# Decoder-trunk step: last eight gelu chunks gated in PSUM and used first, x issued behind the silu, second norm's column sum ahead of three modulation rows

## The reference

```
mod = silu(c) @ w_mod + b_mod                       # six vectors of 1024 for each of 9 sequences
h   = RMSNorm(x) * (1 + scale1) + shift1
x   = x + gate1 * (mixer(h) @ w_out)                # short convolution and mLSTM heads
h   = RMSNorm(x) * (1 + scale2) + shift2
# PEER: 8 heads pick 16 of 128*128 single-neuron experts each, by product keys
a   = einsum(u_tab[picked], h)
y   = einsum(gelu(a) * gate, v_tab[picked])
out = RMSNorm(x + gate2 * y)
```

## Time and profile before

| what | value |
| --- | --- |
| median of 3 runs | 1741.51 us |
| profiled execution | 1741.11 us, span 1739.4 us |
| TensorE busy | 1680.4 us, 97% of the span |
| VectorE, GpSimd, ScalarE busy | 68%, 65%, 38% |
| mean granted TensorE clock | 0.985 |
| DMA | 467.58 MB, mean 269 GB/s |

### The profile page before, as it was taken

One profiled execution on the slowest core, in us unless ns is written; L12 is line 12 of the kernel. 1 busy time (PEld: TensorE's weight loads), 2 busy tenths in 40 slices (PEclk: granted clock), 3 DMA queues, 4 the chain that ended last, 5 costly groups with the idle time before them and its releaser, 6 DMA issues.

```text
span 1739.4 us, 27374 instructions
## 1 busy us (share of the span) xinstructions
PE 1680.4 (97%) x10559; PEld 1609.5 (93%) x10559; DVE 1180.1 (68%) x2322; ACT 667.0 (38%) x1063; POOL 1122.3 (65%) x676
## 2 busy tenths in 40 slices
PE   7999999798999999989999999999999999999996
PEld 3899888596999999989999999998999999999996
DVE  4340244635678789999887788445888888878855
ACT  2454213233334333333343334344444444444432
POOL 1767322121334888977666766776989799999962
PEclk9999999799999999999999999999999999999998
DMA  8645223123223899979999999998999999999951
GB/s 270 213 153 158 73 74 108 45 86 133 74 74 108 276 297 292 330 269 330 354 342 348 346 353 342 342 382 317 406 399 405 365 401 405 404 404 403 403 204 64
DMA packets 197314, 467.58 MB, mean 269 GB/s; under 512 B 21696, under 2 KB 103616, under 8 KB 197056
## 3 DMA queue, kind: packets, MB, share of 16 engines
q1 hardware_dynamic: 82176, 245.46, 40.3%
q0 software_dynamic: 46080, 167.79, 25.6%
q10 hardware_dynamic: 68928, 52.57, 9.1%
HBM read 410.78 MB, written 54.97 MB: 268 GB/s over the span
## 4 chain that ended last, share of the span: by engine, by line
PE 48%; DVE 4%; DMA 4%; POOL 1%; issue 1%; ACT 0%; SPq 0%; DVEq 0%; ACTq 0%
PE ps L896 43%; PE ps L907 5%; DMA tab<-in_tab 2%; DMA gate_scratch<-stage 1%; DVE ug L1522 1%; POOL tLo L640 1%; DMA gt<-gate_scratch 0%; DVE ps L1532 0%; DVE yo L1765 0%; POOL ug L650 0%; DMA gelu_scratch<-ga 0%; DVE eqb L1634 0%; DVE rs L1763 0%; DVE pick L1621 0%; ACT tHi L1142 0%
## 5 line engine op out<-in xcount | busy, mean ns | idle before, releaser
L640 POOL TENSOR_TENSOR tLo<-tab,tHi 128x1024 fp32r<-128x1024 f32 x256 | 621.5, 2428 | 172.0 <-ACT tHi L1142 169.2
L1142 ACT CAST tHi<-tab 128x1024 fp32r<-128x1024 f32 x256 | 268.1, 1047 | 287.1 <-PE ps L896 179.5
L896 PE MATMUL ps<-hHi,tLo 128*128 128x384 f32 x1024 | 351.6, 343 | 2.2 <-ACT ga L1197 1.5
L896 PE MATMUL ps<-actHi,tLo 128*128 128x384 f32 x1024 | 343.3, 335 | 5.5 <-issue 2.9
L896 PE MATMUL ps<-hHi,tHi 128*128 128x384 f32 x1024 | 345.1, 337 | 0.0
L896 PE MATMUL ps<-hLo,tHi 128*128 128x384 f32 x1024 | 344.1, 336 | 0.0
L896 PE MATMUL ps<-actLo,tHi 128*128 128x384 f32 x1024 | 342.7, 335 | 0.0
L896 PE MATMUL ps<-actHi,tHi 128*128 128x384 f32 x1024 | 342.7, 335 | 0.0
L628 POOL TENSOR_TENSOR wLo<-raw,wHi 128x1024 fp32r<-128x1024 f32 x53 | 127.8, 2411 | 309.5 <-ACT wHi L978 309.5
L1522 DVE SCALAR_TENSOR_TENSOR ug<-ug,ps 128x1024 f32<-128x1024 f32 x160 | 191.0, 1218 | 52.7 <-DMA ug<-in_urows,eidx 51.7
L1197 ACT ACTIVATE ga<-ps 128x384 f32<-128x384 f32 x128 | 62.8, 491 | 384.8 <-PE ps L896 374.2
(11 more groups left out here) (346 smaller groups left out, 2471.1 us busy)
## 6 DMA issues: line engine op xcount, KB each, us to landing
tab<-in_tab SPq DMA_DIRECT2D x256, 512.0 KB, 6.6
raw<-in_w SPq DMA_DIRECT2D x101, 512.0 KB, 3.8
gelu_scratch<-ga ACTq DMA_DIRECT2D x128, 192.0 KB, 5.8
gate_scratch<-stage ACTq DMA_DIRECT2D x48, 512.0 KB, 8.4
gt<-gate_scratch SPq DMA_DIRECT2D x32, 768.0 KB, 7.6
gin<-gelu_scratch SPq DMA_DIRECT2D x128, 192.0 KB, 10.2
ug<-in_urows,eidx POOLq DMA_INDIRECT x160, 6.7
ug<-in_vrows,eidx POOLq DMA_INDIRECT x160, 7.7
```

What stands on the lines that cost most here:

```text
L640: pool.tensor_tensor(tLo[:, n % SPL], tab[:, n % TABS], tHi[:, n % SPL].bitcast(F32), ALU.subtract).then_inc(s_tlo, 1)
L896: last = mm(ps[:, bank, 0:TD], w, x[:, k, 0:TD], start=first, stop=end)
L1142: nc.scalar.copy(tHi[:, n % SPL], tab[:, n % TABS]).then_inc(s_thi, 1)
```

## The change

Three places are edited.

1. At the start ScalarE first waits for the conditions c and applies the silu, and issues the four transfers of x behind it. TensorE's wait for the two constants moves from ahead of the first `mod_rows` to behind the second.
2. In the second norm `square_sum(1)` moves from behind `mod_columns(20)` to behind `mod_rows(20)`; on ScalarE `rms(1)` moves ahead of `mod_rows_out(21)`.
3. The last eight chunks (120 to 127) become the first group of the second half. Their gelu is written straight to PSUM bank 4 or 5, and `act_32` works on it there: for them no store, no load and no `gelu_copy`. The other 120 chunks follow in order. The host rolls the groups of `v_tab` by one, and the gate rows are read with an offset. Product 128 no longer waits for a whole group: its matmuls with k wait for `s_alo` 1 + k, and it waits for `s_gelu` NCH + 1 only. SyncE waits for the stores of 120 chunks instead of 128.

```diff
             pe.wait_ge(s_silu, 1)
             for m in range(NMA):
                 mod_rows(m)
+                if m == 1:
+                    pe.wait_ge(s_const, 2)
...
             mod_rows(NMS)
+            square_sum(1)
             mod_rows(NMS + 1)
             mod_columns(NMS)
-            square_sum(1)
...
-            def product(n, hi_in, lo_in, bank):
+            def product(n, hi_in, lo_in, bank, ready=None):
...
+                    if ready is not None:
+                        pe.wait_ge(s_alo, ready + k)
...
-            pe.wait_ge(s_gelu, NCH + 2)
+            pe.wait_ge(s_gelu, NCH + 1)
             for n in range(NCH, NT):
                 g = (n - NCH) // GRP
-                if n % GRP == 0:
+                if n % GRP == 0 and g:
                     pe.wait_ge(s_alo, GRP * (g + 1))
...
-                product(n, actHi[g % 2], actLo[g % 2], late_bank(n))
+                product(n, actHi[g % 2], actLo[g % 2], late_bank(n), None if n > NCH else 1)
...
-            for i in range(KT // 2):
-                act.dma_start(xT[:, 2 * i:2 * i + 2], a["xT"][:, 2 * i:2 * i + 2]).then_inc(s_x[i], 16)
             act.sem_inc(s_gelu, 2)
             act.wait_ge(s_cond, 16)
             f(cT[:], cT[:], ACT.Silu).then_inc(s_silu, 1)
+            for i in range(KT // 2):
+                act.dma_start(xT[:, 2 * i:2 * i + 2], a["xT"][:, 2 * i:2 * i + 2]).then_inc(s_x[i], 16)
...
             mod_rows_out(NMS)
+            rms(1)
             mod_rows_out(NMS + 1)
-            rms(1)
...
             for n in range(NCH):
                 act.wait_ge(s_prod, n + 1)
-                if n >= 3:
+                direct = n - N_DIRECT
+                if direct == 0:
+                    act.wait_ge(s_gev, 2 * NSTEP)
+                if direct >= 2:
+                    act.wait_ge(s_alo, direct - 1)
+                if direct < 0 and n >= 3:
                     act.wait_ge(s_gas[n % 3], 16 * (n // 3))
-                f(ga[n % 3][:], ps[:, n % 2, 0:TD], ACT.Gelu_apprx_tanh).then_inc(s_gelu, 1)
+                f(ga[n % 3][:] if direct < 0 else ps[:, 4 + n % 2, 0:TD], ps[:, n % 2, 0:TD], ACT.Gelu_apprx_tanh).then_inc(s_gelu, 1)
...
-                if n >= NCH - GRP:
-                    c = n - NCH + GRP
-                    if c == 0:
-                        gelu_copy(0)
-                    gelu_copy(c + 1)
-                    act_hi(c)
+                if direct == GRP - 1:
+                    gelu_copy(GRP)
+                if direct >= 0:
+                    act_hi(direct)
...
             def act_32(c):
 
-                v.wait_ge(s_gcp, c + 1)
+                if c < GRP:
+                    v.wait_ge(s_gelu, N_DIRECT + c + 3)
+                else:
+                    v.wait_ge(s_gcp, c - GRP + 1)
```

More of the change, by code:

```diff
@@ L75 @@
 GATE_BANKS = (4, 5, 7)
+N_DIRECT = NCH - GRP
 N_FOLD = NCH + 40
@@ L555, in gates_back @@
                     sp.wait_ge(s_alo, 4 * (q - 1))
-                sp.dma_start(gt[:, q % 2], gt_dram[q].rearrange("p b (c t) -> p b c t", c=4)).then_inc(s_gt[q % 2], 16)
+                sp.dma_start(gt[:, q % 2], gt_dram[(q + N_DIRECT // 4) % (NCH // 4)].rearrange("p b (c t) -> p b c t", c=4)).then_inc(s_gt[q % 2], 16)
             sp.wait_ge(s_out, 160)
@@ L569, in _ @@
                 table(n)
-                gelu_back(n - NCH + 8)
                 if n == NCH - 2:
@@ L573, in _ @@
             for b in range(3):
-                sp.wait_ge(s_gas[b], 16 * len(range(b, NCH, 3)))
+                sp.wait_ge(s_gas[b], 16 * len(range(b, N_DIRECT, 3)))
             gates_back(2)
@@ L578, in _ @@
                 table(n)
-                c = n - NCH + 8
+                c = n - NCH + GRP
                 if c < NCH:
-                    gelu_back(c)
+                    gelu_back(c - GRP)
                     if c % 4 == 3 and c // 4 + 1 < NCH // 4:
@@ L726, in mod_columns @@
                 last.then_inc(s_modt, 1)
-            pe.wait_ge(s_const, 2)
             pe.wait_ge(s_silu, 1)
@@ L1144, in gelu_copy @@
             def gelu_copy(c):
[L1146 to L1150, removed]
+                act.wait_ge(s_gin[c % 4], 16 * ((c - GRP) // 4 + 1))
+                act.wait_ge(s_alo, c - 1)
                 nc.scalar.copy(ps[:, 4 + c % 2, 0:TD], gin[:, c % 4]).then_inc(s_gcp, 1)
@@ L1194, in _ @@
                 act.wait_ge(s_prod, n + 1)
-                if n >= 3:
+                direct = n - N_DIRECT
[4 more added lines that the diff above has]
+                if direct < 0 and n >= 3:
                     act.wait_ge(s_gas[n % 3], 16 * (n // 3))
-                f(ga[n % 3][:], ps[:, n % 2, 0:TD], ACT.Gelu_apprx_tanh).then_inc(s_gelu, 1)
+                f(ga[n % 3][:] if direct < 0 else ps[:, 4 + n % 2, 0:TD], ps[:, n % 2, 0:TD], ACT.Gelu_apprx_tanh).then_inc(s_gelu, 1)
                 t_hi(n + 3)
-                act.wait_ge(s_gelu, n + 3)
-                act.dma_start(ga_dram[n], ga[n % 3][:]).then_inc(s_gas[n % 3], 16)
+                if direct < 0:
+                    act.wait_ge(s_gelu, n + 3)
+                    act.dma_start(ga_dram[n], ga[n % 3][:]).then_inc(s_gas[n % 3], 16)
                 if n == N_SHUF - 2:
@@ L1803 @@
         "tab": np.concatenate([i["u_tab"][0].reshape(NCH, P, KT, P).transpose(0, 3, 2, 1).reshape(NCH, P, D),
-                               i["v_tab"][0].reshape(NCH // GRP, GRP, P, KT, P).transpose(0, 3, 2, 1, 4).reshape(NCH, P, D)]),
+                               np.roll(i["v_tab"][0].reshape(NCH // GRP, GRP, P, KT, P), 1, axis=0)
+                               .transpose(0, 3, 2, 1, 4).reshape(NCH, P, D)]),
         "urows": i["u_tab"][0],
```

## The result

The changed kernel takes 1735.31 us (median of 11 executions, 1726.78 to 1743.06). The kernel before, on the same chip at the same time, takes 1745.38 us (1740.17 to 1754.95). The ratio is 0.9942 with a 95% interval from 0.9917 to 0.9968: faster by 10.1 us, between 5.6 and 14.5. The forecast of a gain holds and its size of 13.3 us is inside the interval, but the time, 1727.8 us with 1723 to 1734 around it, is not: the level was wrong. The profiled executions hide the gain altogether (1741.11 us before, 1740.63 us after), and that is the thread to pull.

The account below looks back on a forecast made before the run. TensorE, busy 1680.4 of 1739.4 us, was taken as the bound, so only its idle or low-clock stretches could move the end. Gains of 2.9 + 5.2 + 5.2 = 13.3 us from 1741.11 us gave 1727.8 us, range 1723 to 1734.

Parts of the forecast that it names:

- The level: Whole kernel: forecast from the profiled execution, 1741.11 us, with the median 0.4 us above it, giving 1727.8 us.
- The start: First weight tiles ahead of x: TensorE starts at about 6.3 us, 3.5 us earlier; gain 2.9 us, bounds 0 and 3.6.
- The second norm: Column sum 4.7 us earlier, query projection at 419.5 us, 6.0 us earlier; gain counted 5.2 us, bounds 3.7 and 6.3.
- The middle: Between the halves: product 128 without its 2.94 us wait, product 132 5.4 us earlier; gain 5.2 us, bounds 1.9 and 5.9.
- table 132 was in time: Rival, between the halves: table 132 as late as before, gain there only 1.9 us, 1731.1 us in all; chance 0.13.
- Sum: Whole kernel: 2.9 + 5.2 + 5.2 = 13.3 us gained, 1727.8 us.
- the gates' loads did not give the middle back: Rival, second half: full DMA or busy GpSimd sets the pace and takes that gain back, 1733.0 us; chance 0.10.
- the start gave something: Rival, kernel start: no gain, as x and tiles five and six share the engines as before, 1730.7 us; chance 0.10.
- chunks 120 to 127 show no wait for their gelu: Rival, eight direct chunks: TensorE waits for gelu in their PSUM ring, 21.6 us slower, 1749.4 us; chance 0.04.

Follow-up runs that it names:

- third trace of the changed kernel: The changed kernel unaltered, run again for another profile against the kernel before; the profiled execution took 1729.96 us.
- its second trace: The kernel before, unaltered, run once more for its profile; the profiled execution took 1752.96 us.

## Why the prediction was wrong, step by step

- **The level: the step that failed.** "I forecast from the profiled one" and "I take a gain at one place to reach the end unless another resource is full there". The trace of before was one of the first, cheaper pattern, near the fastest of 69 executions (median 1748.0); the three of before that I had went up to 1750.05 us, and I took no notice. Of the 7.5 us between 1727.8 and 1735.31 us, 4.3 are this base (1745.38 us beside the result, for 1741.11), and 3.2 are a gain smaller than forecast, which is inside its interval. In the retrieval a resource was full: VectorE, 19.76 of 20 us, with a wait of 2.69 us for `best` behind it. I had read it as something that "waits for TensorE again", so that a shift of both would pass; it does pass when both keep their pattern (7.6 us at the transposes in the third trace of the changed kernel), and 7 to 8 us are lost when the pattern is the other one.
- **The start: 2.9 us, measured 1.2 to 1.7.** The first matmul came nearly as forecast (6.3 us forecast, 6.58 measured). The delay of the steps behind it was sized at 0.3 to 0.7 us, and is 2.1 (3.24 less 1.15). I let the last of tiles and x land near 16.2 us "in either order"; tile six landed at 18.05 us (16.57 before). With x issued 2 us later, from 2 to 7 us the DMA engines moved 303 GB/s where before they moved 362, so the order was not without a price. The forecast also took tiles beside x to need up to 8 us; they needed up to 11.8 before, as the view above shows. In the first trace after, the start's gain went for a time at 187 us, where the clock was 0.52 for 3.5 us (1.00 before): 1.13 us ahead became 0.40 behind, and at 400 us it was 0.83 ahead again.
- **The second norm: 5.2 us, measured 6.2.** The order of steps, the last wait and the projection (419.5 us forecast, 418.51 measured) held. What I took off for a low clock, 0.8, was not needed: the waits went, and the clock stayed at 1.00.
- **The middle: 5.2 us, measured 5.6** (5.17 us earlier than before right in front of product 128 and 10.74 us at product 132, in the third trace of the changed kernel). Product 128 behaves as forecast: in the first trace after, the eighth `act_lo` ends at 1184.39 us and the 22nd matmul, which waits for it, starts at 1185.03. SyncE issued the second gate load only at 1184.4 us, 3 us behind the forecast, and table 132 was in time all the same. The 2.4 us that are lost in front (a wait for gelu 1.8 us longer than before's, and a low clock behind it) are no cost of the change: before itself waits 3.26 us there in its second trace, and the norm's part and the start's part alone wait 3.04 and 2.94:

```profile
1152.51 0.44 PE L896 MATMUL ps<-hHi,tLo 128*128 128x384 f32 x1 [3.26 <-ACT ga L1197]
```

- **Sum.** 1.5 + 6.2 + 5.6 = 13.3 us, less the 2.4 us of luck in the first trace of before, is 10.9; the third trace is 11.2 us shorter. That the sum is the 13.3 us of the forecast is in part luck: the start was over by 1.4 us, the norm and the middle under by 1.0 and 0.4. Set against the median of the 69, 1748.0, the 13.3 us give 1734.7 us.
- **The rivals.** None of the four happened: the gates' loads did not give the middle back, the start gave something, table 132 was in time, chunks 120 to 127 show no wait for their gelu (the wait at product 120 is for chunk 118's). The one that I lacked is a loss between VectorE and GpSimd that comes and goes with the execution.

Open: why an execution falls into one pattern or the other, and whether the norm's part changes the odds (of the four traces without it three show the first pattern, of the four with it one). Eight traces are too few, and the distribution of the changed kernel's 18 executions has no gap from which to count.

## What to carry to other kernels

Before a gain is summed up to the end, look at the next place where another engine is busy for nearly all of a window and TensorE already waits for it; moving two such meetings back, by one product and by three, took four constants here and was worth about as much as any part of the change. Take two profiles of the kernel before, and place the profiled execution in the distribution of its times, before its span serves as the base of a forecast. And compare traces matmul by matmul: the place where an earlier start is lost stands out at once, while totals of busy time hide it.

## What the runs showed of the hardware

An addition on VectorE with both inputs in SBUF took 3.29 us instead of 0.69 with GpSimd's 2.43 us tLo beside it, and was over 0.56 us after tLo; that VectorE and GpSimd fall into two repeatable patterns, with a wait of 0.56 to 0.59 or of 5.73 to 5.75 us at the same product in four traces each, I had not expected. Transfers that ScalarE and SyncE issue alternately land alternately: x at 10.04, 12.64, 15.24 and 17.84 us, the tiles three to six at 10.36, 12.98, 15.51 and 18.05 us.
